# Diffusion trunk step: the first expert pair's input columns made by 128-wide products with the normalised rows stationary

## The reference, cut to what matters

```python
xp = xp + g1 * mix
xp = xp + g2 * hier_moe(modulate(rms_norm(xp, lp["g_ffn"]), sh2, sc2), lp)
...
xb = h_pad[slot_tok].reshape(n_blocks, MOE_BLOCK, D)
def run_block(args):
    xblk, e = args
    return (jax.nn.silu(xblk @ w1[e]) * (xblk @ w3[e])) @ w2[e]
```

## Time and profile before

| what | value |
|---|---|
| time, median of 3 runs | 1648.43 us (1648.01 to 1649.17) |
| span of the profiled execution (first to last instruction) | 1645.8 us |
| TensorE (PE) busy | 1552.0 us, 94% |
| VectorE (DVE) busy | 814.7 us, 49% |
| ScalarE (ACT) busy | 282.5 us, 17% |
| DMA | 581.94 MB, mean 354 GB/s |

### The profile page before, as it was taken

How to read it: one execution, slowest core, us unless ns; L and a number is a source line. 1 busy time by engine, 2 the same in 40 slices (tenths; PEclk the granted TensorE clock), 3 DMA queues, 4 the chain that set the end, 5 groups by cost and what they waited for, 6 DMA issues and landing times.

```text
span 1645.8 us, 18188 instructions
## 1 busy us (share of the span) xinstructions
PE 1552.0 (94%) x6534; PEld 649.3 (39%) x6579; DVE 814.7 (49%) x1473; ACT 282.5 (17%) x748; POOL 101.4 (6%) x185
## 2 busy tenths in 40 slices
PE   6999999999999999999989889998988989988998
PEld 3446655454434444533333233233233333323323
DVE  4784555762365973524524533543443442552444
ACT  3124222122231000110210110111011011011010
POOL 1013100000121000000000000000000000000000
PEclk9999999999999999999999999999999999999999
DMA  9993521667597782899999999999999999999997
GB/s 391 417 413 149 198 115 71 253 239 307 192 391 303 306 336 100 321 415 390 429 429 427 428 428 427 425 428 427 427 426 424 427 424 422 428 428 428 426 424 303
DMA packets 62126, 581.94 MB, mean 354 GB/s; under 512 B 9217, under 2 KB 10177, under 8 KB 16939
## 3 DMA queue, kind: packets, MB, share of 16 engines
q1 hardware_dynamic: 54848, 557.34, 81.9%
q0 software_dynamic: 5936, 23.23, 3.6%
q10 hardware_dynamic: 1296, 0.77, 0.2%
HBM read 584.07 MB, written 7.05 MB: 359 GB/s over the span
## 4 chain that ended last, share of the span: by engine, by line
PE 67%; DMA 17%; DVE 2%; ACT 1%; issue 1%; SPq 0%; POOL 0%; DVEq 0%; ACTq 0%; POOLq 0%
PE bank L1538 23%; DMA ring<-in_w 17%; PE bank L1267 11%; PE bank L1243 9%; PE bank L1441 7%; PE bank L1569 5%; PE bank L1358 2%; PE bank L1490 2%; PE bank L1125 1%; PE bank L1333 1%; PE bank L1588 1%; DVE r L2113 1%; PE bank L1513 1%; PE bank L1341 1%; PE bank L1551 1%
## 5 line engine op out<-in xcount | busy, mean ns | idle before, releaser
L1538 PE MATMUL bank<-ring,r 128*64 128x512 f32 x1920 | 445.7, 600 | 4.6 <-DMA ring<-in_w 4.6
L1569 PE MATMUL bank<-ring,mod_row 128*64 128x512 f32 x896 | 214.0, 633 | 49.6 <-DMA ring<-in_w 41.7
L1538 PEld LDWEIGHTS bank<-ring,r 128*64 128x64 f32 x1920 | 126.6, 136 | 256.3 <-issue 256.2
L1267 PE MATMUL bank<-ring,r 128*128 128x384 f32 (+2 forms) x672 | 225.5, 494 | 0.0
L2378 DVE TENSOR_TENSOR bank<-bank,r 128x512 f32<-128x512 f32 x180 | 125.3, 696 | 105.5 <-PE bank L1441 105.4
L1243 PE MATMUL bank<-ring,r 128*128 128x512 f32 x384 | 170.3, 595 | 0.0
L1267 PEld LDWEIGHTS bank<-ring,r 128*128 128x128 f32 x672 | 123.6, 190 | 91.4 <-issue 43.7
L1569 PEld LDWEIGHTS bank<-ring,mod_row 128*64 128x64 f32 x896 | 77.9, 145 | 176.0 <-issue 165.9
L1441 PE MATMUL bank<-r 128*128 128x512 bf16 x495 | 132.2, 381 | 7.2 <-issue 7.2
L2380 DVE TENSOR_TENSOR r<-r,bank 128x512 f32<-128x512 f32 x180 | 123.7, 687 | 6.2
L2403 DVE TENSOR_SCALAR gains<-bank,w_now 128x512 f32<-128x512 f32 x30 | 22.5, 751 | 204.2 <-PE bank L1569 194.7
(11 more groups left out here) (306 smaller groups left out, 1282.0 us busy)
## 6 DMA issues: line engine op xcount, KB each, us to landing
ring<-in_w SPq DMA_DIRECT2D x174, 2048.0 KB, 17.9
ring<-in_w_mod SPq DMA_DIRECT2D x48, 1024.0 KB, 14.9
ring<-in_w SPq DMA_DIRECT2D x29, 1024.0 KB, 13.0
ring<-in_w_scale SPq DMA_DIRECT2D x16, 1024.0 KB, 21.9
ring<-in_w_shift SPq DMA_DIRECT2D x16, 1024.0 KB, 20.6
ring<-in_w_low SPq DMA_DIRECT2D x16, 1024.0 KB, 7.6
ring<-in_w_o SPq DMA_DIRECT2D x16, 1024.0 KB, 6.7
r<-mod_d POOLq DMA_DIRECT2D x8, 1024.0 KB, 7.6
```

Source lines behind the costliest of these rows:

```text
L1267: mm = pe.matmul(acc[acc_of(a)][:, 0:w], h_t[:, k, t * P:(t + 1) * P], wu[:, j, :], start=(k == 0), stop=(k == KD - 1))
L1538: mm = pe.matmul(ps[64 * c:64 * c + 64, :], xg_t[:, j, 64 * c:64 * c + 64], big_cut(slot_of(u), (8, 512))[:, j % 8, :], start=(j == 0), st ...
L1569: mm = pe.matmul(y_ps[c][64 * h:64 * h + 64, :], act_t[:, f, 64 * h:64 * h + 64], big_cut(slot_of(u), (2, D))[:, c % 2, f * 512:(f + 1) * ...
```

## The change

`pick` swaps its operands. The stationary operand is now a 128-column slice of the tile's rows, `h2[:, t, 4b+i::16]` (token by feature, every 16th feature), and the slot table of 128 columns moves: four products of 128x128 by 128 columns in the place of one of 128x128 by 512. The result is already the columns [feature p, slot] for step j = 4b+i, so the copy to `xg`, the 16 transposes of `turn_picked` and their semaphore are gone. ScalarE copies all four banks straight to `xg_t` (VectorE's two copies go) once `h2_ready` is at 5, and the first pair's w1 product waits for `picked` at j = 0, 4, 8 and 12. GpSimd's wait for `pick_turned` before the first gather is gone. The counts in the other waits on `xt_read_a` and `xt_read_v` are lowered by 2.

```diff
--- before.py
+++ after.py
@@ -729,7 +729,7 @@
             "oh_ready", "rank_full", "vals_ready", "tab_full", "tab_ready"))
         gidx, xg_in, xt_full, xt_read_a, xt_read_v = (sem(n) for n in (
             "gidx", "xg_in", "xt_full", "xt_read_a", "xt_read_v"))
-        picked, pick_turned, w_ready = sem("picked"), sem("pick_turned"), sem("w_ready")
+        picked, w_ready = sem("picked"), sem("w_ready")
         h1_full, h3_full, sg_ready, act_ready, at_full, at_read_a, at_read_v = (sem(n) for n in (
             "h1_full", "h3_full", "sg_ready", "act_ready", "at_full", "at_read_a", "at_read_v"))
         y_full, y_read_a, y_read_v = sem("y_full"), sem("y_read_a"), sem("y_read_v")
@@ -1218,20 +1218,13 @@
 
             def pick(t, b):
 
-                mm = pe.matmul(pick_ps[b][:, :].rearrange("q (p i) -> q p i", i=4),
-                                 at_first[:, t, :, :].rearrange("p h s -> p (h s)"),
-                                 h2[:, t, :].rearrange("q (p j) -> q p j", j=KD)[:, :, 4 * b:4 * b + 4],
-                                 start=(t == 0), stop=(t == TILES - 1))
+                for i in range(4):
+                    mm = pe.matmul(pick_ps[b][:, i * P:(i + 1) * P], h2[:, t, 4 * b + i::KD],
+                                   at_first[:, t, :, :].rearrange("p h s -> p (h s)"),
+                                   start=(t == 0 and i == 0), stop=(t == TILES - 1 and i == 3))
                 if t == TILES - 1:
                     mm.then_inc(pick_full, 1)
                 return mm
-
-            def turn_picked(b):
-
-                pe.wait_ge(picked, b + 1)
-                for i in range(4):
-                    mm = pe.transpose(pick_ps[b][:, i * P:(i + 1) * P], xg[:, 512 * b + i:512 * b + 512:4], ident)
-                mm.then_inc(pick_turned, 1)
 
             def out_part(a, cc, t, i):
 
@@ -1415,11 +1408,8 @@
             pick(2, 1)
             pe.wait_ge(h2_ready, 4)
             pick(2, 2)
-            turn_picked(0)
             pe.wait_ge(h2_ready, 5)
             pick(2, 3)
-            for b in range(1, 4):
-                turn_picked(b)
 
             def turn_x(half):
                 for b in range(2):
@@ -1472,8 +1462,8 @@
 
             for w, ps in enumerate((h1_ps, h3_ps)):
                 for j in range(KD):
-                    if w == 0 and j in (0, 4, 8, 12):
-                        pe.wait_ge(*((xt_read_v, j // 8 + 1) if j % 8 == 0 else (xt_read_a, j // 8 + 1)))
+                    if w == 0 and j % 4 == 0:
+                        pe.wait_ge(picked, j // 4 + 1)
                     if w == 0 and j == 12:
                         pe.wait_ge(vals_ready, 1)
                         for c in range(ASSIGN):
@@ -1503,8 +1493,8 @@
             pe.wait_ge(tab_ready, 1)
             for c in range(4):
                 if c == 2:
-                    pe.wait_ge(xt_read_a, 4)
-                    pe.wait_ge(xt_read_v, 4)
+                    pe.wait_ge(xt_read_a, 2)
+                    pe.wait_ge(xt_read_v, 2)
                 first_arrived(16 + 2 * c)
                 first_arrived(17 + 2 * c)
                 for f in range(4):
@@ -1521,8 +1511,8 @@
 
             def up(m, backs=BACKS, last=False):
 
-                pe.wait_ge(xt_read_a, m * 2 + 4)
-                pe.wait_ge(xt_read_v, m * 2 + 4)
+                pe.wait_ge(xt_read_a, m * 2 + 2)
+                pe.wait_ge(xt_read_v, m * 2 + 2)
                 for w, ps in enumerate((h1_ps, h3_ps)):
                     for j in range(KD):
                         ua, ub = 4 * w + j // 8 * 2, 4 * w + j // 8 * 2 + 1
@@ -1558,8 +1548,8 @@
                 turn_act(m)
                 for c in range(4):
                     if c == 2:
-                        pe.wait_ge(xt_read_a, m * 2 + 6)
-                        pe.wait_ge(xt_read_v, m * 2 + 6)
+                        pe.wait_ge(xt_read_a, m * 2 + 4)
+                        pe.wait_ge(xt_read_v, m * 2 + 4)
                     if c % 2 == 0:
                         moe_arrived(8 + c, m)
                         moe_arrived(9 + c, m)
@@ -1822,13 +1812,11 @@
             e.activation(g_s, g_s, ACT.Exp).then_inc(cond_ready, 1)
             e.wait_ge(re_in, 1)
             e.activation(r_, d_, ACT.Exp).then_inc(re_out, 1)
+            e.wait_ge(h2_ready, 5)
             for b in range(4):
                 e.wait_ge(pick_full, b + 1)
-                e.activation(xg[:, 512 * b:512 * b + 512], pick_ps[b][:, :], ACT.Copy).then_inc(picked, 1)
-            for b in (1, 3):
-                e.wait_ge(pick_turned, b + 1)
                 e.activation(xg_t[:, 4 * b:4 * b + 4, :].rearrange("p a b -> p (a b)"), pick_ps[b][:, :],
-                             ACT.Copy).then_inc(xt_read_a, 1)
+                             ACT.Copy).then_inc(picked, 1)
             front(-1)
             parts(-1, 0, False)
             parts(-1, 2, True)
@@ -2286,10 +2274,6 @@
                             ALU.subtract).then_inc(ge_in, 1)
             v.tensor_tensor(d_, m1, m0, ALU.subtract).then_inc(re_in, 1)
 
-            def picked_out(b):
-                v.wait_ge(pick_turned, b + 1)
-                v.tensor_copy(xg_t[:, 4 * b:4 * b + 4, :].rearrange("p a b -> p (a b)"), pick_ps[b][:, :]).then_inc(xt_read_v, 1)
-
             rank, exp_a, ovb, q_, slot_a, item_a, tmp6 = (asg[:, i, :] for i in range(1, 8))
             weight = asg[:, 0, :]
             v.wait_ge(rank_full, 2)
@@ -2315,9 +2299,6 @@
             after(v.tensor_reduce(q_, beyond[:, 0:ASSIGN, :], AX, ALU.add))
             after(v.scalar_tensor_tensor(out=slot_a, in0=q_, scalar=-float(CAP), in1=rank, op0=ALU.mult, op1=ALU.add))
             v.tensor_scalar(slot_a, slot_a, 1.0, None, ALU.add)
-            picked_out(0)
-            picked_out(2)
-
             after(v.tensor_tensor(tmp6, ovb, q_, ALU.add))
             after(v.scalar_tensor_tensor(out=tmp6, in0=tmp6, scalar=float(EXPERTS - 1), in1=exp_a,
                                          op0=ALU.add, op1=ALU.subtract))
@@ -2623,7 +2604,6 @@
             g.dma_start(tokens, ins["consts"][:, n_const:n_const + T]).then_inc(tokens_in, 16)
             for t in range(TILES):
                 g.wait_ge(*h2_out[t])
-            g.wait_ge(pick_turned, 4)
             g.wait_ge(tab_ready, 1)
             after(g.tensor_copy(gat_now[:], row_tab[:, 1:2]))
             gather()
```

## The result

The changed kernel is slower: 1658.81 us (median of 4 runs, 1656.01 to 1661.40) against 1648.68 us for the kernel before, ratio 1.0059 with a 95% interval of 1.0047 to 1.0071. I had forecast 1646.8 us and a range up to 1650.4 us. The direction and the size are those of my second rival at its upper end.

A forecast was written before the change was run, and what follows sets the result against it. The weight stream bounds the kernel, its start set by TensorE: 12.52 us removed less 10.9 added gives 1.6 us; span 1645.8 - 1.6 = 1644.2, plus 2.6 to the runs' median, 1646.8 us; range 1645.2 to 1650.4 us.

The forecast's parts named there:

- Rival 2: Picks' scattered weight loads don't hide: 0.167 or 0.22 us a record, giving 1651.9 or 1657.0 us; chance 0.12.
- What bounds the kernel: Weight stream sets the end; TensorE before the w1 product sets SyncE's issue at 756.59 us, ending a 2.6 us DMA loss.
- rival 1: DMA queue ahead of the expert loop: the gain dies there, the stream's start stays, 1648.4 us; chance 0.15.
- What goes: On TensorE's path, 16 turns (1.91 us) and twelve picks of 512 columns (10.61 us) are removed: 12.52 us.
- What comes: New picks on TensorE: 96 records of 128 columns at 0.113 us, 10.9 us; ends 10.5 and 21.1 us.
- the step doubles the 103 ns: Worst reading of the picks' weight load: step 16 doubles its column time, about 0.22 us a record.
- The two add: Reading of the picks' weight load: step and fp32 product costs add, 55 ns more, 0.167 us a record.
- The two page rules: Skill rules against the change: 16-byte SBUF line crossings are penalised; loads overlap matmuls only across row groups, else about 0.22 us a record.
- break-even: Pick record time from which rival 2 decides: 12.52/96 = 0.130 us a record.
- Edits at nothing: ScalarE's wait and copies, VectorE's dropped copies, SyncE's units and the gather around the picks were costed at no time.
- Units 14 and 15: SyncE loads waiting for pick(0,3) and pick(1,3): 0.1 to 0.2 us later, ahead of an already full queue.
- The gain if the load hides: TensorE starts the w1 product 1.6 us earlier, near 696.8 us, and all 1.6 us reach the stream.

The follow-up runs named there:

- contiguous slices: Changed kernel with picks taking 128 neighbouring elements as stationary operand, wait for tile 2's last part before its first pick: 1648.67 us against 1648.51, ratio 1.0000.
- pairs of neighbours: Changed kernel with normalised rows kept so features of steps 2a and 2a+1 are neighbours, TensorE loading with a step of 2: 1648.06 against 1648.51 us, ratio 1.0000.
- the kernel with the scattered moving operand: Kernel before, with the 512 moving columns of a pick reordered to lie 16 elements apart: 1658.22 against 1648.69 us, ratio 1.0059.
- Step 2: Changed kernel, picks' stationary operand taken with steps of 1, 2, 4, 8 elements for b = 0 to 3: +3.7 us (one run); step 2 records 0.119 us.

## Why the prediction was wrong, point by point

- **What bounds the kernel.** Right for a delay: where a kernel was timed more than once, +8.4 us in the stage gives +8.5 and +10.1 in the time, and +9.8 gives +9.5. A gain is shown only as far as the issue of 756.59 us. With contiguous slices and with pairs of neighbours that issue lies at 755.83 and 755.78 us, 0.8 us earlier, much as their w1 product starts earlier (697.75 and 697.59 us for 698.44), and the DMA engines are 80% and 84% busy in 754 to 760 us where they were 69%. So the first step of rival 1, that the issue gains nothing, did not happen. Whether the gain reaches the end is open: the four stages between -1.1 and -0.6 us give times of -0.5 to +1.1 us, inside the scatter.
- **What goes**, 12.52 us: right.
- **What comes**, 96 x 0.113 = 10.9 us, is the step that failed. Measured 96 x 0.22 = 21.1 us. The number of records was right and so was the pitch of a contiguous load (0.113 and 0.112 us in three experiments); mis-sized was the scattered load. I had its price in the earlier trace rows: the columns of a transpose's load cost 54 ns contiguous and 109 ns scattered, a doubling. I named "the step doubles the 103 ns: about 0.22 us" as the worst end and took 0.113, because L1428 and L1233 stream at 0.113 and 0.121 us. That pitch was no evidence. The columns of a transpose's load take 109 ns even when they double, about the pitch that its matmul sets by itself: with contiguous loads, in the kernel with the scattered moving operand, twelve turns take 1.34 us, 0.112 each. So the doubling doesn't show in the pitch. The product's load starts from twice the length (103 ns) and comes out at 223 ns, twice its matmul. The load durations told it, the pitches hid it. (The matmuls of 0.275, 0.277 and 0.284 us in that working, and VectorE's copies of 0.68 us, are in the trace but not among the lines of the earlier trace rows.)
- **"The two add", 0.167 us:** wrong as well; the step multiplies: 223 ns for the columns of a load, not 103 + 55.
- **The two page rules.** I set down SBUF — State Buffer, section "Door 1", of the Trainium skill as a penalty without a size and left out the part of its sentence that gives the threshold, at least two hits per line. Step 2 and the pairs bear this out, with two elements in each line at no cost, and the size for one element a line is a factor of two. TensorE: Matmul & The Clock Gate, section "The mechanism", is contradicted for these products: a load of 296 ns hides beside a matmul that uses the same 128 rows of the array (0.447 us a record). That this rule gave 0.22 us too, the value that was measured, was luck: the load doubles, it doesn't wait its turn.
- **Rival 2** (0.12): came true at its upper size. Nothing contradicts its break-even of 0.130 us a record: step 2 (0.120 in the kernel with pairs) gives a shorter stage; no kernel lies close above it. Its 8.6 us of delay was 8.4.
- **Edits at nothing.** ScalarE's wait and copies: right, the w1 product follows the last pick with no wait, in the slow kernel too. Units 14 and 15 "0.1 to 0.2 us later": unit 14 goes out at 693.73 us in the place of 689.41 and unit 15 at 700.95 in the place of 693.12, 4.3 and 7.8 us later. 1.0 us of each is the offset of that run, the rest the longer picks that they wait for. Unit 16, which was to stay at 703.68 us, goes out at 711.88.
- **The gain if the load hides**, 1.6 us: in the contiguous kernel the stage shrinks by 1.0 us, with 0.41 us of waiting for tile 2 that the changed kernel's order of waits may not have. That all of 1.6 us would come without it isn't shown.
- **The range** ended at 1650.4 us, although the forecast rested on an operation that no row showed and one of its two load readings alone meant 8.6 us. A chance of 0.12 for it was too small.

## What to carry to other kernels

When a product is re-oriented to save a copy and a transpose, look at what both operands look like in SBUF: here 128 fp32 elements 8 bytes apart were free on either side, 12 bytes apart they cost half as much again (tried on the stationary side only), and from 16 bytes on they cost the double on either side. With 128 moving columns nothing hides a load of double length; with 512 it hid all but 0.01 us. Take the price of a load from the load records, not from the pitch of a stream in which something else is as long.

## What the runs showed of the hardware that I had not expected

- The price goes by 16-byte lines touched, once there are fewer than two elements in each: records of 0.111, 0.119, 0.175, 0.234, 0.240 and 0.219 us for steps of 1, 2, 3, 4, 8 and 16 fp32 elements. That 4 and 8 are dearer than 16 stays unexplained.
- It holds for TensorE's stationary and moving operands, and for VectorE in both directions (2.02 and 2.01 against 1.29 us for 1024 elements), and two elements in each line are free in all three places where they were tried: moving columns (0.115 and 0.113 us), VectorE's reads (0.480 us for 256 elements), and the step of 2 in the stationary operand (0.119 us).
